# One of six parts of a modulation vector moved from TensorE to VectorE in a two-block transformer kernel

## The reference, cut to what matters

```
c_act = jax.nn.silu(c)                              # (1, 1024)
mod = (c_act @ w_ada[l] + b_ada[l])[:, None, :]     # w_ada: 1024 x 6144
shift1, scale1, gate1, shift2, scale2, gate2 = jnp.split(mod, N_MOD, axis=-1)
h = _rmsnorm(x, g_mix[l]) * (1.0 + scale1) + shift1
proj = h @ w_in[l]
...
y = jnp.concatenate([y_a, y_b, y_c], axis=-1) @ w_out[l]
x = x + (1.0 + gate1) * y
h = _rmsnorm(x, g_ffn[l]) * (1.0 + scale2) + shift2
up = _causal_dwconv(h @ w_up[l], conv_w[l], conv_b[l])
```

## Time and profile before

| | us |
|---|---|
| median of 3 runs | 936.97 |
| lowest, highest | 934.45, 938.82 |
| profiled execution | 938.96 |
| its span, first to last instruction | 937.2 |
| DVE busy in the span | 612.9 |
| ACT busy in the span | 497.1 |

### The profile page before, as it was taken

One profiled execution on the slowest core, in us unless ns is written; L12 is line 12 of the kernel. 1 busy time (PEld: TensorE's weight loads), 2 busy tenths in 40 slices (PEclk: granted clock), 3 DMA queues, 4 the chain that ended last, 5 costly groups with the idle time before them and its releaser, 6 DMA issues.

```text
span 937.2 us, 17329 instructions
## 1 busy us (share of the span) xinstructions
PE 909.5 (97%) x7189; PEld 841.5 (90%) x7189; DVE 612.9 (65%) x958; ACT 497.1 (53%) x729; POOL 0.2 (0%) x4
## 2 busy tenths in 40 slices
PE   5899999999999999999999999999999999999997
PEld 2688878899999999778999999999999999988886
DVE  0565676787776776787766555566986765566664
ACT  4427674755555567665633443446656653344333
POOL 0000000000000000000000000000000000000000
PEclk9799999999999999989999999999999999999999
DMA  9988757675456569414465555555442655555541
GB/s 351 358 286 279 275 187 237 217 258 195 174 176 222 180 166 178 107 47 131 138 208 184 188 195 196 189 168 176 135 152 91 224 174 161 199 186 180 181 135 45
DMA packets 130889, 176.38 MB, mean 188 GB/s; under 512 B 20816, under 2 KB 108412, under 8 KB 130812
## 3 DMA queue, kind: packets, MB, share of 16 engines
q1 hardware_dynamic: 129852, 173.12, 56.6%
q10 hardware_dynamic: 960, 2.16, 0.6%
HBM read 174.22 MB, written 1.05 MB: 187 GB/s over the span
## 4 chain that ended last, share of the span: by engine, by line
PE 81%; DVE 8%; ACT 5%; DMA 3%; issue 3%; SPq 0%; ACTq 0%; DVEq 0%
PE psum L1616 24%; PE psum L1608 20%; PE psum L1609 20%; PE psum L1612 4%; PE psum L1613 4%; DMA raw<-in_w_ada_dram 2%; DVE w_lo L967 2%; PE psum L1710 1%; ACT w_hi L534 1%; DMA raw<-in_w_in_dram 1%; PE psum L2215 1%; PE psum L2144 1%; PE psum L1726 1%; ACT arena L815 1%; DVE small L1424 1%
## 5 line engine op out<-in xcount | busy, mean ns | idle before, releaser
L534 ACT ACTIVATE w_hi<-raw 128x2048 fp32r<-128x2048 f32 (+1 forms) x139 | 264.4, 1904 | 146.9 <-PE psum L1616 122.4
L1608 PE MATMUL psum<-h_hi,w_hi 128*128 128x256 f32 x1352 | 329.9, 283 | 1.5 <-DVE h_lo L1139 1.1
L967 DVE TENSOR_TENSOR w_lo<-raw,w_hi 128x2048 fp32r<-128x2048 f32 (+1 forms) x139 | 313.1, 2277 | 22.9 <-ACT w_hi L534 22.9
L1609 PE MATMUL psum<-h_lo,w_hi 128*128 128x256 f32 x1352 | 325.7, 280 | 0.0
L1608 PEld LDWEIGHTS psum<-h_hi,w_hi 128*128 128x128 f32 x1352 | 254.8, 188 | 11.0 <-issue 8.0
L1609 PEld LDWEIGHTS psum<-h_lo,w_hi 128*128 128x128 f32 x1352 | 256.1, 189 | 0.8
L1616 PE MATMUL psum<-h_hi,w_lo 128*128 128x256 f32 x1352 | 187.0, 280 | 1.0 <-DVE w_lo L967 0.9
L1616 PEld LDWEIGHTS psum<-h_hi,w_lo 128*128 128x128 f32 x1352 | 170.0, 188 | 1.9 <-DVE w_lo L967 1.6
L1335 DVE SCALAR_TENSOR_TENSOR arena<-psum,rstd 128x256 f32<-128x256 f32 x64 | 26.8, 423 | 132.3 <-PE psum L1616 130.4
L1608 PE MATMUL psum<-a_hi,w_hi 128*128 128x256 f32 x464 | 110.7, 280 | 0.6 <-DVE a_lo L1322 0.4
L1609 PE MATMUL psum<-a_lo,w_hi 128*128 128x256 f32 x464 | 110.3, 279 | 0.0
(11 more groups left out here) (272 smaller groups left out, 899.6 us busy)
## 6 DMA issues: line engine op xcount, KB each, us to landing
raw<-in_mlp_w_in_dram SPq DMA_DIRECT2D x32, 1024.0 KB, 5.7
raw<-in_mlp_w_out_dram SPq DMA_DIRECT2D x32, 1024.0 KB, 7.2
raw<-in_w_ada_dram SPq DMA_DIRECT2D x24, 1024.0 KB, 7.9
raw<-in_w_up_dram SPq DMA_DIRECT2D x22, 1024.0 KB, 5.1
raw<-in_gla_w_in_dram SPq DMA_DIRECT2D x12, 1024.0 KB, 5.4
raw<-in_w_down_dram SPq DMA_DIRECT2D x11, 1024.0 KB, 5.8
raw<-in_w_in_dram SPq DMA_DIRECT2D x10, 1024.0 KB, 7.2
raw<-in_w_out_dram SPq DMA_DIRECT2D x4, 1024.0 KB, 5.7
```

What stands on the lines that cost most here:

```text
L534: act.activation(chunk(w_hi, m % SPLIT_SLOTS, SPLITS[m]), chunk_raw(r % RAW_SLOTS, SPLITS[m]), ACT.Copy).then_inc(*mark("w_hi", m))
L967: dve.tensor_tensor(chunk(w_lo, m % SPLIT_SLOTS, key), chunk_raw(r % RAW_SLOTS, key), chunk(w_hi, m % SPLIT_SLOTS, key).bitcast(F32), ALU. ...
L1608: pe.matmul(dst, high, both[0], start=start, stop=False, skip_group_check=True)
L1609: return pe.matmul(dst, high, both[1], start=False, stop=False, skip_group_check=True)
```

## The change

Part 4 is no longer summed by TensorE. In its four steps DVE multiplies each block of weight rows by the condition value of its row (one value per partition) and adds it into `ada`, 128x1024: one TENSOR_SCALAR for the first block, seven SCALAR_TENSOR_TENSOR for the rest, each of which waits for the one ahead. The ring slots of part 4 are released by DVE (`ada_scaled`). After `out 0` a new step `fold` sums the partitions: four matmuls with ones, each 256 columns into a column group of 32. ACT copies 256 columns instead of 512, two transposes remain of four, and DVE makes the result in one addition.

```diff
+ON_DVE = (4,)
...
-    s += [("gains", 1), ("project", "out", 0), ("project", "out", 1), ("project", "out", 2), ("mod", 4),
+    s += [("gains", 1), ("project", "out", 0), ("fold", 4), ("project", "out", 1), ("project", "out", 2), ("mod", 4),
...
                     if old[0] == "ada":
-                        sp.wait_ge(*at("ada_added", *old[1:]))
+                        sp.wait_ge(*at("ada_scaled" if old[1] in ON_DVE else "ada_added", *old[1:]))
...
-                if q == 3:
+                if q == 3 and p not in ON_DVE:
                     act.wait_ge(*at("ada_added", p, 3))
...
+            def fold(p):
+
+                act.wait_ge(*at("job", "fold", p))
+                act.activation(ada[:, p % 2, 0:S], bank("fold", p)[:, 0:S], ACT.Copy).then_inc(*mark("act_read", "fold", p))
...
+                if p in ON_DVE:
+                    folded = bank("mod", p)[:, 0:S:32].rearrange("p (b g) -> p g b", g=4)
+                    dve.tensor_tensor(mod[:, KT * p:KT * p + KT].rearrange("p (g b) -> p g b", b=2), folded,
+                                      col("b_ada", KT * p, KT).rearrange("p (g b) -> p g b", b=2), ALU.add)\
+                        .then_inc(*mark("dve_read", "mod", p))
+                    return
...
+            def ada_step(p, q):
+
+                if p not in ON_DVE:
+                    return
+                r, total = LOAD_OF[("ada", p, q)], ada[:, p % 2, :]
+                dve.wait_ge(*landed(r))
+                if q == 0:
+                    dve.wait_ge(*at("c_act", 0))
+                    dve.wait_ge(*at("job", "mod", p - 2))
+                for kk in range(2):
+                    k, src = 2 * q + kk, wview(raw, r % RAW_SLOTS, 2)[:, kk, :]
+                    if k == 0:
+                        ins = dve.tensor_scalar(total, src, c_rep[:, 0, 0:1], None, ALU.mult)
+                    else:
+                        dve.wait_ge(*(at("ada_scaled", p, q - 1) if kk == 0 else at("ada_half", p, q)))
+                        ins = dve.scalar_tensor_tensor(out=total, in0=src, scalar=c_rep[:, k, 0:1], in1=total,
+                                                       op0=ALU.mult, op1=ALU.add)
+                    ins.then_inc(*(mark("ada_scaled", p, q) if kk else mark("ada_half", p, q)))
...
             def ada_step(p, q):
 
 
+                if p in ON_DVE:
+                    return
                 r = LOAD_OF[("ada", p, q)]
...
-                pe.wait_ge(*at("act_read", "ada", p))
+                pe.wait_ge(*(at("act_read", "fold", p) if p in ON_DVE else at("act_read", "ada", p)))
                 dst = take(pe, "mod", p)
-                for b in range(4):
+                for b in range(2 if p in ON_DVE else 4):
...
+            def fold(p):
+
+                pe.wait_ge(*at("ada_scaled", p, 3))
+                dst = take(pe, "fold", p)
+                for g in range(4):
+                    ins = pe.matmul(dst[32 * g:32 * g + 32, 0:S], cst("ones")[:, 0:32], ada[:, p % 2, g * S:g * S + S],
+                                    start=True, stop=True, skip_group_check=True)
+                ins.then_inc(*mark("job", "fold", p))
```

More of the change, by code:

```diff
@@ L940, in finish @@
                         .then_inc(*mark("out_left_landed", t, by=16))
-            steps = {"setup": setup, "ada": ada_sums, "turn_x": turn_x, "angles": angles, "root": root, "round": round_first, "shift": shift, "first": first, "scaled": scaled,
+            steps = {"setup": setup, "ada": ada_sums, "fold": fold, "turn_x": turn_x, "angles": angles, "root": root, "round": round_first, "shift": shift, "first": first, "scaled": scaled,
                      "split": split, "silu": silu, "unscaled": unscaled,
@@ L1570, in _ @@
             steps = {"setup": setup, "rows": columns, "angles": angles, "w_sp": mask_w_sp, "in": take_in, "down": down, "qkv": qkv,
-                     "gla": gla, "mlp_up": mlp_up, "mod": modulation, "gains": gains, "normed": all_normed, "round_low": round_low, "first": first, "scaled": scaled, "rope": rope,
+                     "gla": gla, "mlp_up": mlp_up, "mod": modulation, "ada": ada_step, "gains": gains, "normed": all_normed, "round_low": round_low, "first": first, "scaled": scaled, "rope": rope,
                      "v_norm": v_norm, "gate_mix": gate_mix, "stick_a": stick_a, "stick_b": stick_b,
@@ L2226, in _ @@
             steps = {"setup": setup, "rows": turn_rows, "turn_x": turn_x, "w_sp": turn_w_sp, "ada": ada_step, "shift": shift, "in_part": in_part,
-                     "mod": modulation,
+                     "mod": modulation, "fold": fold,
                      "in": take_in, "rope": rope,
```

## The result

The changed kernel takes 948.83 us (median of four runs, 946.79 to 949.99), the kernel before 937.49 in the same comparison (median of four, 934.45 to 938.82). The ratio is 1.0123, 95% interval 1.0091 to 1.0155: slower by 11 us. The forecast was 951.0 with a range of 944.0 to 957.5.

A forecast was written before the change was run, and what follows sets the result against it. Bound: the late-released ring slot and the ACT and DVE queues behind it, not TensorE alone. 6.8 + 2.6 - 1.0 + 2.6 + 0.2 (fold) = +11.2, plus 3 for the clock: 951.2 us against the median 936.97; range 944 to 957.5.

The forecast's parts named there:

- What bounds: From 97 to 137 us TensorE, 97% busy, is not the only bound; none of its 4.0 us saved counts as gained.
- The slot, +6.8: Step 4,0 on DVE frees its ring slot late; the load of `in 10` goes out at 114.1, not 107.29: +6.8 us.
- The price of a sum: DVE at 128x1024: 0.76 us for the first sum, 1.3 for each other, 9.9 us in all.
- 4,1 hidden: Step 4,1 on DVE ends at 116.5 and the wait for `in 10` hides it: no cost.
- 4,2 +2.6: Step 4,2 stands behind w_lo of `in 10`, where DVE's timeline is dense until the mask of stick 5: +2.6 us.
- the idle -1.0: DVE's 0.99 us idle before w_lo of `out 0` is absorbed because DVE now comes last: -1.0 us.
- 4,3 +2.6: Step 4,3 stands between w_lo of `out 0` and the stick weights, with no cover: +2.6 us.
- The clock, +3: TensorE's clock falls after new idles and slows short matmuls before `out 0` and `out 0` itself: 1 to 5 us, taken as +3.
- rival (a): The chain without the clock: short matmuls keep 2.4 GHz, 936.97 + 11.2 = 948.2 us; chance 0.30.
- (b): TensorE is the bound and DVE's 35% idle hides the sums: 933.2 us, not slower; chance 0.05.
- (c): Only the two late sums count; ACT absorbs the late landing, 2.6 to 5.2 us remain, 940 to 942; chance 0.06.
- (d): The clock falls in both places and stays: +18 to +22 us, over 955; chance 0.10.

The follow-up runs named there:

- late_slot: Kernel before, part 4 still on TensorE; only the load of `in 10` is held until DVE has finished w_lo of `in 9`: 942.42 us, +6.2 against before.
- all_moved: Changed kernel with all eight sums on DVE moved to places where DVE stood idle: 938.82 us, +2.3 against the kernel before.
- all_held: all_moved plus six dummy matmuls filling TensorE's 3.10 us idle ahead of `gate_mix`: 938.58 us, +1.9 against the kernel before.
- thin_sums: Kernel before with part 4's TensorE matmuls cut from 512 to 32 columns, nothing put elsewhere: 935.85 us, -0.6, ratio 0.9995.
- third_held: third_moved plus seven dummy matmuls filling TensorE's idle ahead of the second `stick_c`: 947.60 us, +11.1 against the kernel before.
- last_moved: Changed kernel with step 4,3 on DVE moved behind the last mixer output, before w_lo of `out 1`: 946.85 us, +10.7 against the kernel before.
- filler: Changed kernel plus 28 dummy matmuls in TensorE's 4.8 us idle behind `stick_a` of stick 4: 948.68 us, +12.2 against the kernel before.
- third_moved: Changed kernel with step 4,2 on DVE moved ahead of the masks of sticks 2 and 3: 950.28 us, +14.1 against the kernel before.
- ring_after: Changed kernel with another load order, `in 9` and `in 10` one load earlier, DVE steps following that order: 942.26 us, +5.6 against the kernel before.
- first_moved: Changed kernel with steps 4,0 and 4,1 moved into DVE's idle time before v_norm's product: 942.33 us, +6.1 against the kernel before.
- first_held: first_moved plus six dummy matmuls on TensorE ahead of `gate_mix`: 941.25 us, +4.6 against the kernel before.

## Why the prediction was right

The range held the time and the direction was right. The mechanism is shown by late_slot (a slot 4.1 us late costs 6.2 us, an estimated 3.4 without the clock) and by all_moved (the same work, without the late slot and out of the full queue, costs 2 us). That the measured 948.83 lies within 1 us of the sum without the clock, 948.2, is in part luck: the term of the slot was 0.6 us too high, and 0.9 us at the last store of the result (see all_held) stands in no term, and the two nearly cancel. By its steps:

- **What bounds.** That the engine totals mislead was the core of it, and thin_sums puts a number to it: 3.2 us of matmuls taken off an engine that is 97% busy are worth 0.6 us, if anything, and at most 1.8. No run here has them gone with the clock held.
- **The slot, +6.8.** The load went out 6.2 us later (113.49 against 107.29), w_lo of `in 10` came 6.1 us later (124.76 against 118.69). The 0.6 too much: w_lo of `in 9` began 0.4 us earlier than before, and 4,0 was a little shorter (0.74 + 1.28 us).
- **The price of a sum.** TENSOR_SCALAR 0.74 us (0.76 forecast), SCALAR_TENSOR_TENSOR 1.275 to 1.287 with a median of 1.285 (1.28, taken as 1.3 with the handover). A formula of the Trainium skill, "VectorE: DVE Perf Modes", section "The TRN2 errata — SBUF-src ops pay a fixed extra latency per instruction", gives (N + 151)/0.96 ns for an fp32 `tensor_tensor` addition, by which I estimate 1.22 us at 1024 columns; the kernel before has 1.217 for such an operation, so the trace agrees. The measured two-tensor operation with a scalar from SBUF takes 60 ns more.
- **4,1 hidden, 4,2 +2.6, the idle -1.0, 4,3 +2.6.** Each as forecast: DVE idles 4.35 us behind 4,1; 2.60 us each for the others; the 0.99 us is gone. 6.1 + 2.6 - 1.0 = 7.7 for w_lo of `out 0`, where the trace has 136.22 - 128.71 = 7.5; with 4,3 and 0.35 for the fold (0.2 forecast) the sum is 10.5, and with the 0.9 at the last store, which I had not reckoned with, 11.4. The times differ by 11.3, with 3 us of uncertainty to either side. Two moves show that 4,2 and 4,3 are not worth 2.6 us each by themselves: taken away one at a time, another wait takes their place after 0.7 us (third_held) or 2.19 (last_moved), so the terms add up only in this order of work. The first matmul of `out 0` came at 147.20, a little ahead of the 148 to 151 that I had named as a sign, since neither the clock's part nor the whole term of the slot came.
- **The load's duration.** The chain of the changed kernel has 5.21 us for the load of `in 10`, 5.3 before. The 6.15 us for 1 MB of the Trainium skill, "DMA: Bandwidth & Descriptors", section "Measured", given there for loads issued from GpSimd, are 0.9 more than the trace shows for this one from SyncE; the number of the row was the right one to use.
- **The clock, +3: this step failed.** The clock stood at half from 121 to 128 only, covered by DVE, and filler shows that part to cost nothing; from 129 to the end of the mixer it was whole, so nothing of the +3 was paid. The case that came is rival (a), the chain without the clock, 948.2, to which I had given 0.30 against 0.48. Its idles were 2.27 and 2.19 us, where I had reckoned with 4 and 2.4: TensorE was through with stick 4 at 134.1, not at 133, having run a part of `in 10` at half clock, and the mask of stick 5 came 0.8 us sooner than forecast. The effect itself is real one change away: third_moved, last_moved and ring_after have it in that part of the mixer, and third_held prices it at 3 us.
- **The rivals (b), (c) and (d)** did not come. (b) asked for a slot no more than 1.6 us late. It was 6.2, and late_slot shows that 4.1 is paid in full already, less only DVE's idle of 0.99.

## What to carry to other kernels

Before moving work to an engine with idle time, write down whose buffer slot it holds and what stands behind it in that engine's queue: here the same eight instructions cost 11 us in one place and 2 in another, while what they relieved was worth 0.6 us, if anything. When two loads of one ring make an engine wait, try their order first; one line of it gave 2 to 3 us. Read the start and the end of the trace too, and not only the stretch that was changed: 0.9 us of this change stands at the last store. And after every edit look at the granted clock behind each new idle of TensorE: a gain on another engine can come back as a loss.

## What the runs showed of the hardware

- TensorE's clock fell to 1.2 GHz during or just behind idles of 2.81, 3.10, 3.28, 3.63, 4.81 and 5.36 us, and eight short matmuls of 128x256 then took 1.55 us in place of 0.87. The length of the idle alone does not tell. Ahead of `gate_mix` it fell behind 2.34 us in thin_sums, 2.70 in filler and 2.77 in last_moved, and not behind 2.58 us in the changed kernel; at 135 us in first_moved it did not fall behind 3.08.
- Work of no use that fills such an idle pays where TensorE is the last to come (third_held, 3 us; first_held, 0.9 of the stretch; all_held, 1.5 of the stretch, though only 0.4 of the time) and brings nothing where another engine is (filler, 0).
- The clock's other falls move from execution to execution. At 414 us it fell for 7 us in the traces of before and all_held, at the same place (423 us) in third_held, for half as long in thin_sums, and in no other; the DVE splits on either side of that place (382 and 432 us in before) lie 49.8 to 49.9 us apart with a fall of 7 us and 47.8 in all other traces, 2 us less. The fall at 25 us lasted 10 us in five traces, where the 88x88 matmul then stood at 74.4 to 75.6, and 7 us in the nine others, where it stood at 73.0 to 73.9. I estimate from them that these two places make up 3 to 4 of the up to 5.6 us by which times of one kernel spread.
- Not all of the spread is the clock: in the traces of the changed kernel and of all_held the part from 293 to 555 us behind `out 0` took 1.6 us more than in all others (263.2 against 261.6), at a granted clock of 1.00. The cause is open.
